# SSD step sizes in the first round of the input projection, with their weights stationary, in a hybrid SSD, Hyena and MoE block

## The chip, the cores and the metric

The kernel runs on one core of a Trainium2 chip. The metric is the device time of one execution in microseconds (us). TensorE multiplies (its weight loads are rows of their own, PEld), VectorE (DVE) and ScalarE (ACT) do elementwise work, GpSimd (POOL) a little of it, SyncE (SP) issues the large DMAs. The engines run their instruction lists in order and meet at semaphores; a list can wait only for its own next instruction.

## The reference, cut to what matters

One layer of a backbone: adaLN-modulated RMSNorm of 256 latent and 256 context tokens of width 2048, one input projection, an SSD (Mamba-2) branch and a Hyena branch, a gated merge, and a mixture of experts. The change touches the SSD step sizes: 64 of the projection's columns (2 directions x 32 heads), a softplus, and the cumulative sums from which all decays come.

```python
def dt_pair(dt_raw, dt_bias):
    bsz, L, _ = dt_raw.shape
    return jax.nn.softplus(dt_raw.astype(F32).reshape(bsz, L, 2, SSD_HEADS) + dt_bias.astype(F32))
...
    dt = dt_pair(p[..., COL_DT:COL_HY], lp['ssd_dt_bias'])
    a = -jnp.exp(lp['ssd_a_log'].astype(F32))
    yf, hf = ssd_chunked(xs, dt[:, :, 0], a[0], bm, cm, h0f)
    yb, hb = ssd_chunked(flip(xs), flip(dt[:, :, 1]), a[1], flip(bm), flip(cm), h0b)
...
    # in ssd_chunked, chunks of 128 tokens
    xd = (xs.astype(F32) * dt[..., None]).reshape(bsz, nc, Q, G, R, P)
    ad = (dt * a).reshape(bsz, nc, Q, G, R).transpose(0, 3, 4, 1, 2)
    acs = jnp.cumsum(ad, axis=-1)
    decay_in = jnp.exp(jnp.where(lower, acs[..., :, None] - acs[..., None, :], -jnp.inf))
    decay_to_end = jnp.exp(acs[..., -1:] - acs)
```

## The kernel before

The program is a row of stages. Each is a block with one instruction list per engine, and between two stages all engines meet at a barrier. No scheduler is at work: the order on each engine is the order in which the code is written. Three stages matter.

**Norm stage (to 127 us).** It leaves the modulated tokens, transposed, as `h_hi` and `h_lo`: fp32 values split into a rounded part and the rest, for 16 tiles of the width (`kt`) and 2 x 256 tokens. A product in full precision is then three matmuls on rounded values, `mm3` (lines 195 to 197): hi with hi, hi with lo, lo with hi.

**xBC projection (127 to 388 us, lines 522 to 680).** Weights come as slabs of 512 KB through 8 slots, `raw`, which SP's `feed` fills as they come free. ScalarE rounds a slab (`split_hi`, L185) into one of 4 places of `w_hi`, which waits for TensorE to have used the slab 4 before (`w_used`). VectorE takes the difference into `w_lo` (`split_lo`, L189), and TensorE waits for that (`lo_ready`). There are 6 rounds of 8 slabs; a round has two parts `p` of 4 slabs, and `project(i, p)` does 24 matmuls of 512 columns for each slab into banks `2p` and `2p + 1`. Then ScalarE copies the two banks out into `p2_pad` (`copy_out`), VectorE convolves (`conv`, L646 and L651), ScalarE applies silu (L601, L603), TensorE transposes (`turn`, L559) into banks 4 to 7 and VectorE copies them to `xb` (`tokens`). The first round is written out (`body(0, first=True)`), rounds 1 to 4 are a hardware loop, and the last round, again written out, has only the 256 latent tokens. In each of these lists the later steps of round i - 1 stand among the splits of round i. VectorE, for one, has slabs 0 to 3, then the steps of the round before, then slabs 4 to 7 and `conv(i, 0)`. SP loads the step weights `wdt` (128 x 16 x 64) at the head of the stage, and does nothing else with them here.

**Scan stage (from 388 us, lines 735 to 1055).** At its head, before any group, stand the step sizes. SP loads the bias, `a_log` and `d` (`bc`). ScalarE rounds `wdt` into place 3 of `w_hi` (L873), VectorE takes the rest (L927). TensorE multiplies with the tokens stationary and the weights moving, 4 tiles of tokens x 16 `kt` x 3 matmuls of 64 columns, so that the steps come out with tokens on the partitions. VectorE and ScalarE take turns for the softplus (L934 to L949, L877 to L881) and leave the steps `dtr` and their product with `a`, `adr` (L951). TensorE multiplies `adr` with triangular tables for the cumulative sums (L783, and L800, L801 for the sums over a whole part), VectorE and ScalarE make exponentials `ex` of them (L957 to L963, L884, L885).

Then a loop over the 4 head groups: copies of the group's part (`bg` L975 and `xsg` L976 on VectorE, `bgt` L889 and `cgt` L890 on ScalarE), small matmuls for states and outputs (L816 to L833), exponentials, mixing (L1024) and 64-column matmuls within a chunk (L854). Between them `ada(part)` reads 32 slabs of `ada_w` in each group (L263, 128x512 with 32 stationary columns): the adaLN rows that later stages need. `feed` refills `raw` for them. ScalarE and GpSimd write these rows out at the end of each group.

Of the kernel before, what the change touches and what calls it, by code (L numbers as in the profile page):

```python
# [199 lines left out]
def build(nc, io, consts):  # L200
    ctx = ExitStack()
    with ctx:
# [102 lines left out]
        with nc.Block() as block:  # L305
# [210 lines left out]
        acc = place("p2_acc", [P, 2, CH_XC], at=after("p2_pad"))  # L516
        s = Box()
        (s.padded, s.conved, s.silud, s.turned, s.tok_copied, s.zeroed,
         s.wdt) = sems(
            "p2", "padded", "conved", "silud", "turned", "tok_copied", "zeroed", "wdt")  # L520

        with nc.Block() as block:

            @block.sync
            def _(sp):
                sp.dma_start(wdt[:], w_in[:, :, COL_DT:COL_HY]).then_inc(s.wdt, 16)
                st.feed(sp, 6, 8, xbc_src, st.lo_ready, lambda j: ada_src(2, j))
                sp.wait_ge(s.wdt, 16)

            @block.gpsimd  # L530
            def _(pool):
                pool.memset(pad[:], 0.0).then_inc(s.zeroed, 1)

            @block.tensor
            def _(pe):
# [3 lines left out]
                def project(i, p, both):  # L539
                    pe.wait_ge(s.padded, i * 4 + 2 * p + 2)  # L540
                    n = 512 if both else L
                    for q in range(4):
# [9 lines left out]
                        mm.then_inc(st.w_used, 1)  # L552

# [17 lines left out]
                body(0, first=True)  # L571
                with pe.Fori(1, 5) as i:
                    body(i)
# [3 lines left out]
            def _(act):  # L577
# [27 lines left out]

                def body(i, first=False, last=False):
# [3 lines left out]
                    for j in (1, 2):  # L610
                        st.split_hi(act, i, 8, j)
                    if not first:
                        copy_out(i - 1, 1, True)
# [4 lines left out]
                    for j in (5, 6):  # L618
                        st.split_hi(act, i, 8, j)
                    copy_out(i, 0, not last)  # L620
                    st.split_hi(act, i, 8, 7)

# [9 lines left out]
            def _(dve):  # L632
# [33 lines left out]

                def body(i, first=False, last=False):
                    for j in range(4):
                        st.split_lo(dve, i, 8, j)
                    if not first:  # L670
                        tokens(i - 1, 0)
                        conv(i - 1, 1, True)
                    for j in range(4, 8):
                        st.split_lo(dve, i, 8, j)
                    if not first:
                        tokens(i - 1, 1)
                    conv(i, 0, not last)

# [35 lines left out]
        wdt_hi, wdt_lo = k.w_hi[:, 3, :], k.w_lo[:, 3, :]  # L714
        xw = place("p3_xw", [P, 6, GC], at=after("wdt"))
        dtr = place("p3_dt", [P, 4, 64], at=after("p3_xw"))
        adr = place("p3_ad", [P, 4, 64], at=after("p3_dt"))
        ex = place("p3_ex", [P, 8, 64], at=hi0 + 3 * 4 * SUB)
# [1710 lines left out]
```

## Time and profile before

| | us |
|---|---|
| median of 3 runs | 2642.38 (2639.52 to 2642.42) |
| the profiled execution | 2643.38 |
| its span, first to last instruction | 2641.6 |
| norm stage ends | about 127 |
| barrier between xBC projection and scan stage | about 388.4 |
| first matmul of the group loop | 453.26 |
| first instruction of the next stage | 652.4 |

Over the whole span TensorE is busy 88% of the time, VectorE 58%, ScalarE 39%, GpSimd 8%, and the mean granted TensorE clock is 0.931 of full speed. These shares are averages over stages with different limits. For this change the timeline of the two stages is to be read, engine by engine, and the windows: for a stretch of the span, how long each engine was busy in it, with how many instructions, the clock that TensorE was granted, the busy share of the 16 DMA engines and what they moved. A granted clock of 1.00 is 2.4 GHz, 0.50 is 1.2 GHz. An fp32 matmul that isn't split into rounded parts stands in the trace as two rows of the same instruction.

### The profile page before, as it was taken

The numbers are of one execution on the slowest core, as the hardware profiler recorded it, in microseconds if no ns is written. First come the engines' busy times: TensorE is split into PE (matmuls) and PEld (weight loads), VectorE is DVE, ScalarE is ACT, GpSimd is POOL, SyncE is SP. The second block draws the span as 40 slices with busy tenths as digits, with TensorE's granted clock in tenths as the row PEclk, the third lists the DMA queues.
The fourth block names the chain that finished last, engine by engine and source line by source line (L and its number), as shares of the span: only waits on it lengthen the run. The fifth ranks groups of instructions, "written<-read, shape, count | busy, mean of one in ns | idle before, by whom it ended". The sixth has DMA issues, their size and how long they took to land. (4 is left out here: it accounts for less than half of the span.)

```text
span 2641.6 us, 34797 instructions
## 1 busy us (share of the span) xinstructions
PE 2334.3 (88%) x12901; PEld 1886.5 (71%) x12901; DVE 1520.1 (58%) x1934; ACT 1032.1 (39%) x1278; POOL 203.6 (8%) x145
## 2 busy tenths in 40 slices
PE   6699988997768798888888999987799999999995
PEld 1288877454658797777777899965588888878773
DVE  1345552565434255767675544453655568989986
ACT  1423321111433242323233333332234446777773
POOL 1000000000000003333333100000000000000000
PEclk9899995998888999999999999998699999999998
DMA  9733320998434553333333456562156668999993
GB/s 370 286 113 93 94 83 22 360 347 308 141 95 155 166 162 100 116 101 116 111 118 105 122 163 183 183 248 59 64 192 191 191 209 320 382 351 365 375 336 129
DMA packets 285401, 503.49 MB, mean 191 GB/s; under 512 B 18757, under 2 KB 158576, under 8 KB 283494
## 3 DMA queue, kind: packets, MB, share of 16 engines
q1 hardware_dynamic: 280310, 481.54, 54.3%
q0 software_dynamic: 4976, 20.43, 2.2%
q8 instruction: 71, 1.16, 0.2%
q14 instruction: 44, 0.36, 0.0%
HBM read 499.78 MB, written 2.13 MB: 190 GB/s over the span
## 5 line engine op out<-in xcount | busy, mean ns | idle before, releaser
L189 DVE TENSOR_TENSOR w_lo<-raw,w_hi 128x1024 fp32r<-128x1024 f32 x720 | 917.8, 1287 | 670.4 <-ACT w_hi L185 643.8
L185 ACT ACTIVATE w_hi<-raw 128x1024 fp32r<-128x1024 f32 x720 | 760.9, 1060 | 842.5 <-PE bank L197 824.4
L195 PE MATMUL bank<-h_hi,w_hi 128*128 128x256 f32 (+1 forms) x1664 | 514.4, 309 | 42.4 <-DVE w_lo L189 29.0
L197 PE MATMUL bank<-h_hi,w_lo 128*128 128x256 f32 (+1 forms) x1664 | 508.1, 305 | 0.0
L196 PE MATMUL bank<-h_lo,w_hi 128*128 128x256 f32 (+1 forms) x1664 | 508.1, 305 | 0.0
L195 PEld LDWEIGHTS bank<-h_hi,w_hi 128*128 128x128 f32 x1664 | 321.0, 193 | 60.0 <-issue 29.5
L196 PEld LDWEIGHTS bank<-h_lo,w_hi 128*128 128x128 f32 x1664 | 320.8, 193 | 14.3 <-issue 1.9
L197 PEld LDWEIGHTS bank<-h_hi,w_lo 128*128 128x128 f32 x1664 | 320.7, 193 | 12.8
L195 PE MATMUL bank<-w_hi,ys_hi 128*128 128x512 f32 x384 | 154.2, 402 | 17.8 <-DVE p_tmp L1855 11.4
L263 PE MATMUL bank<-raw,cpad 128*32 128x512 f32 x768 | 148.9, 671 | 20.5 <-DMA raw<-in_ada_w 20.3
L195 PE MATMUL bank<-ys_hi,w_hi 128*128 128x256 f32 x512 | 148.3, 290 | 17.4 <-ACT merged L1347 10.6
L195 PE MATMUL bank<-w_hi,lt_hi 128*128 128x512 f32 x384 | 154.0, 401 | 2.8 <-DVE w_lo L189 2.8
L196 PE MATMUL bank<-w_lo,ys_hi 128*128 128x512 f32 x384 | 153.5, 400 | 0.0
L197 PE MATMUL bank<-w_hi,ys_lo 128*128 128x512 f32 x384 | 153.4, 399 | 0.0
L197 PE MATMUL bank<-w_hi,lt_lo 128*128 128x512 f32 x384 | 150.0, 391 | 0.0
L196 PE MATMUL bank<-w_lo,lt_hi 128*128 128x512 f32 x384 | 149.7, 390 | 0.0
L196 PE MATMUL bank<-ys_lo,w_hi 128*128 128x256 f32 x512 | 147.4, 288 | 0.0
L197 PE MATMUL bank<-ys_hi,w_lo 128*128 128x256 f32 x512 | 147.4, 288 | 0.0
L195 PE MATMUL bank<-w_hi,hidt_hi 128*128 128x512 f32 x320 | 126.5, 395 | 3.7 <-DVE hidt_lo L2322 2.6
L197 PE MATMUL bank<-w_hi,hidt_lo 128*128 128x512 f32 x320 | 125.3, 392 | 0.0
L196 PE MATMUL bank<-w_lo,hidt_hi 128*128 128x512 f32 x320 | 125.2, 391 | 0.0
L195 PE MATMUL bank<-w_hi,h_hi 128*128 128x512 f32 (+1 forms) x192 | 79.5, 414 | 42.8 <-ACT p_gz L1132 25.1
(358 smaller groups left out, 3103.6 us busy)
## 6 DMA issues: line engine op xcount, KB each, us to landing
raw<-in_w_in SPq DMA_DIRECT2D x240, 512.0 KB, 3.8
raw<-in_ada_w SPq DMA_DIRECT2D x192, 512.0 KB, 7.6
raw<-in_moe_w_gate SPq DMA_DIRECT2D x128, 512.0 KB, 6.0
raw<-in_moe_w_up SPq DMA_DIRECT2D x128, 512.0 KB, 6.0
raw<-in_moe_w_down SPq DMA_DIRECT2D x128, 512.0 KB, 5.9
raw<-in_w_ssd_out SPq DMA_DIRECT2D x32, 512.0 KB, 3.4
raw<-in_w_hy_out SPq DMA_DIRECT2D x32, 512.0 KB, 3.4
raw<-in_w_o SPq DMA_DIRECT2D x32, 512.0 KB, 3.6
```

The source lines that it names most:

```text
L185: act.activation(self.k.w_hi[:, j % HL, :], self.k.raw[:, j % RAW, :], ACT.Copy).then_inc(self.hi_ready, 1)
L189: dve.tensor_tensor(self.k.w_lo[:, j % HL, :], self.k.raw[:, j % RAW, :], self.k.w_hi[:, j % HL, :].bitcast(F32), ALU.subtract).then_inc(s ...
L195: pe.matmul(out, lhs[0], rhs[0], start=start, stop=False)
L196: pe.matmul(out, lhs[0], rhs[1], start=False, stop=False)
L197: return pe.matmul(out, lhs[1], rhs[0], start=False, stop=stop)
L263: mm = pe.matmul(bank[32 * strip:32 * strip + 32, :], k.cpad[:, kt, :], w[:, 0, n * 512:(n + 1) * 512], start=(kt == 0), stop=(kt == KT - 1))
```

## The change

The head of the scan stage moves into the first round of the xBC projection, and the step matmul is turned round.

- SP issues the three loads of `bc` behind that of `wdt`.
- ScalarE rounds `wdt` behind slab 1 into columns 0 to 63 of a new tile `p2_wdt_s` (128 x 16 x 128), VectorE puts the rest into columns 64 to 127.
- TensorE, between slab 0 and slab 1, holds these 128 columns stationary and moves the 512 tokens of `h_hi` and `h_lo` past them: 32 matmuls into bank 5. The outputs stand with steps on the partitions, rounded part and rest apart. VectorE copies the bank out (`dtx`) behind slab 3.
- TensorE, between slab 1 and slab 2, multiplies each 128 tokens of `dtx` with `halves`, two identity matrices one above the other: this adds the two parts and turns them to tokens on the partitions (bank 7). GpSimd makes `halves` from the identity table.
- Softplus behind slab 5 on ScalarE and on VectorE; decay sums between slabs 4 and 5 on TensorE (banks 6 and 7); the rest of the decays at the end of the round on both. TensorE waits for them (`exps`) before round 1.
- The scan stage starts with its group loop; its tiles are placed elsewhere.

```diff
+        wdt_s = place("p2_wdt_s", [P, KT, P], F32R, at=free + 4 * 512)
...
                 sp.dma_start(wdt[:], w_in[:, :, COL_DT:COL_HY]).then_inc(s.wdt, 16)
+                sp.dma_start(bc[:, 0:2, :], io["ssd_dt_bias"].rearrange("a b h -> a (b h)")[0]
...
+                pool.tensor_tensor(halves[:], k.ident[:, 0:64], k.ident[:, 64:P], ALU.add).then_inc(s.zeroed, 1)
...
+                def steps():
+                    pe.wait_ge(s.dt_lo, 1)
+                    for kt in range(KT):
+                        pe.matmul(k.psum[5][:], wdt_s[:, kt, :], k.h_hi[:, :, kt, :], start=(kt == 0), stop=False)
+                        mm = pe.matmul(k.psum[5][:], wdt_s[:, kt, :], k.h_lo[:, :, kt, :], start=False,
+                                       stop=(kt == KT - 1))
+                    mm.then_inc(s.dt_mm, 1)
+
+                def step_tokens():
+                    pe.wait_ge(s.zeroed, 2)
+                    pe.wait_ge(s.dt_sb, 1)
+                    for t in range(4):
+                        mm = pe.matmul(k.psum[7][:, t * 64:(t + 1) * 64], dtx[:, t * P:(t + 1) * P], halves[:],
+                                       start=True, stop=True)
+                    mm.then_inc(s.dt_tok, 1)
+
+                def decay_sums():
+                    pe.wait_ge(s.dts, 1)
+                    out = k.psum[6][:].rearrange("p (n d h) -> p n d h", n=8, d=2)
...
-                    project(i, 0, not last)
+                    project(i, 0, not last, (steps, step_tokens) if first else ())
                     if not first:
                         turn(i - 1, 1)
-                    project(i, 1, not last)
+                    project(i, 1, not last, (decay_sums,) if first else ())
...
                 body(0, first=True)
+                pe.wait_ge(s.exps, 1)
...
+                def step_highs():
+                    act.wait_ge(s.wdt, 16)
+                    act.activation(wdt_s[:, :, 0:64], wdt[:], ACT.Copy).then_inc(s.dt_hi, 1)
...
+                def decay_exps():
+                    act.wait_ge(s.rest, 1)
...
+                def step_lows():
+                    dve.wait_ge(s.dt_hi, 1)
+                    dve.tensor_tensor(wdt_s[:, :, 64:P], wdt[:], wdt_s[:, :, 0:64].bitcast(F32),
+                                      ALU.subtract).then_inc(s.dt_lo, 1)
+
+                def step_copy():
+                    dve.wait_ge(s.dt_mm, 1)
+                    dve.tensor_copy(dtx[:], k.psum[5][:]).then_inc(s.dt_sb, 1)
+
+                def softplus():
+                    dve.wait_ge(s.dt_tok, 1)
+                    dve.wait_ge(s.bc, 48)
...
+                def decay_rest():
+                    dve.wait_ge(s.sums, 1)
...
             def _(pe):
-                pe.wait_ge(s.dt_lo, 1)
-                w = (wdt_hi.rearrange("p (kt n) -> p kt n", n=64), wdt_lo.rearrange("p (kt n) -> p kt n", n=64))
-                for t in range(4):
-                    src, half = t // TT, t % TT
-                    for kt in range(KT):
-                        h = (k.h_hi[:, src, kt, half * P:(half + 1) * P], k.h_lo[:, src, kt, half * P:(half + 1) * P])
-                        mm = mm3(pe, k.psum[0][:, t * 64:(t + 1) * 64], h, (w[0][:, kt, :], w[1][:, kt, :]),
-                                 kt == 0, kt == KT - 1)
-                mm.then_inc(s.dt_mm, 1)
```

Where the order prints names, `p_wdt_s` is the stationary tile, `p_dtx` the copied bank, `p_ad` is `adr`, `p_u` the scratch of the softplus. In the first round on ScalarE, the list before:

```order
L185 ACTIVATE w_hi<-raw 128x1024 [waits w_used,raw_full5]
L185 ACTIVATE w_hi<-raw 128x1024 [waits w_used,raw_full6]
L587 ACTIVATE p_pad<-bank 128x4x64 [waits p2_conved,w_used]
L590 ACTIVATE p_pad<-bank 128x256
L587 ACTIVATE p_pad<-bank 128x4x64
L590 ACTIVATE p_pad<-bank 128x256
L185 ACTIVATE w_hi<-raw 128x1024 [waits w_used,raw_full7]
```

and now, from slab 5 to slab 6 and behind slab 7:

```order
L185 ACTIVATE w_hi<-raw 128x1024 [waits w_used,raw_full5]
L676 ACT_TABLE_LOAD
L676 ACTIVATE p_bc<-p_bc 128x64 [waits p2_bc]
L678 ACTIVATE p_u<-p_dt 128x256 [waits p2_soft]
L680 ACTIVATE p_u<-p_u 128x256 [waits p2_act]
L682 ACT_TABLE_LOAD
L682 ACTIVATE p_u<-p_u 128x256 [waits p2_soft]
L185 ACTIVATE w_hi<-raw 128x1024 [waits w_used,raw_full6]
...
L185 ACTIVATE w_hi<-raw 128x1024 [waits w_used,raw_full7]
L687 ACT_TABLE_LOAD
L687 ACTIVATE p_ex<-bank 128x256 [waits p2_rest]
```

The softplus stands between slabs 5 and 6, and the Exps, which wait for VectorE's `rest`, close the round. On TensorE, what comes into the first round (the plus rows; the matmuls of the projection between them stand as before, and 28 more of the step matmuls are left out):

```order
 L197 MATMUL bank<-h_hi,w_lo 128x512
+L559 MATMUL bank<-h_hi,p_wdt_s 128x512 [waits p2_dt_lo]
+L560 MATMUL bank<-h_lo,p_wdt_s 128x512
...
+L568 MATMUL bank<-p_halves,p_dtx 128x64 [waits p2_dt_sb,p2_zeroed]
+L568 MATMUL bank<-p_halves,p_dtx 128x64 x3
 L195 MATMUL bank<-h_hi,w_hi 128x512 [waits lo_ready]
...
+L579 MATMUL bank<-p_ad,tri 128x32 [waits p2_dts]
+L579 MATMUL bank<-p_ad,tri 128x32 x17
```

Three groups of matmuls now stand between slabs, each behind a wait of its own. On ScalarE at the head of the scan stage and of its group loop, before:

```order
L884 ACT_TABLE_LOAD
L884 ACTIVATE p_ex<-bank 128x256 [waits p3_rest]
L884 ACTIVATE p_ex<-bank 128x128
L885 ACTIVATE p_ex<-p_ex 128x128
L887 UNCONDITIONAL_BRANCH
L887 ISA
L889 ISA [waits p3_ydone]
L889 ACTIVATE p_bgt<-xbc_act 128x256
L890 ISA
L890 ACTIVATE p_cgt<-ct 128x256
```

and now:

```order
L968 UNCONDITIONAL_BRANCH [waits barrier_Pool_Activation_PE_DVE_SP_release]
L971 UNCONDITIONAL_BRANCH
L971 ISA
L973 ISA [waits p3_ydone]
L973 ACT_TABLE_LOAD
L973 ACTIVATE p_bgt<-xbc_act 128x256
L974 ISA
L974 ACTIVATE p_cgt<-ct 128x256
```

The copies follow the barrier directly, and the table load stands inside the loop, behind the group's wait, ahead of its first copy.

## Rows read from the trace of the kernel before

**Rows 1.** Windows: busy us (instructions) of each engine, granted clock, DMA share, GB/s.

```profile
core 0: us, PE busy (x) PEld busy (x) DVE busy (x) ACT busy (x) POOL busy (x), PEclk, DMA share, GB/s
155.00:177.00 22.00, 22.00 (x103) 18.34 (x102) 11.26 (x14) 9.37 (x16) 0.00 (x0) 1.00 0.34 96
...
388.50:432.10 43.60, 41.17 (x192) 41.04 (x192) 1.24 (x2) 2.60 (x3) 1.14 (x2) 0.50 0.01 3
...
440.20:449.80 9.60, 9.55 (x44) 9.46 (x44) 0.00 (x0) 0.00 (x0) 0.00 (x0) 0.50 0.00 0
...
500.00:550.00 50.00, 43.54 (x282) 23.33 (x283) 30.43 (x82) 10.22 (x30) 2.99 (x4) 0.97 0.96 354
```

**Rows 2.** Timeline, head of the scan stage: start, length, engine, work [idle before, releaser].

```profile
388.50 1.06 ACT L873 ACTIVATE w_hi<-wdt 128x1024 fp32r<-128x1024 f32 x1 [0.29 <-PEq L522]
...
432.08 0.42 DVE L934 TENSOR_TENSOR p_dt<-bank,p_bc 128x256 f32<-128x256 f32 x1 [41.27 <-PE bank L197]
...
440.25 7.89 PE L783 MATMUL bank<-p_ad,tri 128*128 128x32 f32 x36 [8.20 <-DVEq L955]
...
451.67 0.41 ACT L890 ACTIVATE p_cgt<-ct 128x256 f32 x1
...
453.26 1.22 PE L816 MATMUL bank<-p_cgt,p_bgt 128*128 128x128 f32 x4 [3.42 <-DVE p_xsg L976]
...
456.60 3.34 SPq L156 DMA_DIRECT2D raw<-in_ada_w  x5
```

**Rows 3.** Timeline of the projection's first round, and the landing time of `wdt`.

```profile
127.02 0.37 SPq L526 DMA_DIRECT2D wdt<-in_w_in  x1
...
DMA to landing us min/median/max: 4.2/4.2/4.2
...
130.51 0.77 PE L195 MATMUL bank<-h_hi,w_hi 128*128 128x512 f32 x1 [24.47 <-DVE w_lo L189]
...
138.21 1.06 ACT L185 ACTIVATE w_hi<-raw 128x1024 fp32r<-128x1024 f32 x1 [6.27 <-PE bank L197]
...
143.65 1.06 ACT L185 ACTIVATE w_hi<-raw 128x1024 fp32r<-128x1024 f32 x1 [4.38 <-PE bank L197]
...
158.73 5.51 DVE L651 SCALAR_TENSOR_TENSOR p_acc<-p_pad,vcol,p_acc 128x528 f32<-128x528 f32 x8
```

**Rows 4.** Timeline: a table load, and the head of the second group.

```profile
433.48 1.28 ACT L881 ACT_TABLE_LOAD   x1
434.77 0.42 ACT L881 ACTIVATE p_u<-p_u 128x256 f32<-128x256 f32 x1
...
500.82 0.40 ACT L890 ACTIVATE p_cgt<-ct 128x256 f32 x1
...
501.33 0.69 DVE L976 COPY p_xsg<-xb 128x1024 f32 x1
...
502.07 0.71 PE L816 MATMUL bank<-p_cgt,p_bgt 128*128 128x128 f32 x4 [2.48 <-DVE p_xsg L976]
```

**Rows 5.** Timeline, TensorE in the first group: two-pass fp32 matmuls of 64 columns.

```profile
481.11 2.00 PE L854 MATMUL bank<-p_xsg,p_mix 128*128 128x64 f32 x16
482.95 0.44 PE L844 MATMUL bank<-tri,p_spans 128*128 128x128 f32 x2
```

**Rows 6.** Timeline, TensorE in the third group; windows of 1 us (columns as rows 1).

```profile
589.49 2.00 PE L854 MATMUL bank<-p_xsg,p_mix 128*128 128x64 f32 x16 [1.35 <-DVE p_mix L1024]
...
592.00:593.00 1.00, 1.00 (x12) 0.27 (x8) 0.14 (x1) 0.00 (x0) 0.00 (x0) 0.50 0.85 336
...
595.00:596.00 1.00, 1.00 (x10) 1.00 (x9) 0.00 (x0) 0.31 (x1) 0.61 (x1) 0.84 0.97 377
...
598.00:599.00 1.00, 0.00 (x0) 0.00 (x0) 0.71 (x2) 1.00 (x4) 0.00 (x0) 0.86 0.69 262
...
605.00:606.00 1.00, 1.00 (x11) 0.12 (x4) 0.29 (x2) 0.00 (x0) 0.00 (x0) 0.72 1.04 422
...
135.00:136.00 1.00, 1.00 (x6) 0.83 (x5) 0.00 (x0) 0.00 (x0) 0.00 (x0) 1.00 1.04 329
```

More of the change, by code:

```diff
@@ new lines, in step_tokens, with total @@
+                def step_tokens():
[8 more added lines that the diff above has]
+                    out = k.psum[6][:].rearrange("p (n d h) -> p n d h", n=8, d=2)
+                    a = adr[:].rearrange("p t (d h) -> p t d h", d=2)
+                    def total(n, d, *terms):
+                        for m, (table, t) in enumerate(terms):
+                            mm = pe.matmul(out[:, n, d, :], table, a[:, t, d, :], start=(m == 0), stop=(m == len(terms) - 1))
+                        return mm
+                    for c in range(TT):
+                        total(c, 0, (k.upper, c))
+                        total(c, 1, (k.lower, c))
+                        total(2 + c, 0, (k.below, c))
+                        total(2 + c, 1, (k.above, c))
+                        for d in range(2):
+                            total(6 + c, d, (k.ones, c))
+                    total(4, 0, (k.upper, 2))
+                    total(4, 1, (k.lower, 2), (k.ones, 3))
+                    total(5, 0, (k.upper, 3), (k.ones, 2))
+                    total(5, 1, (k.lower, 3))
+                    whole = k.psum[7][:, 256:320].rearrange("p (d h) -> p d h", d=2)
+                    for d, (first, second) in enumerate(((3, 2), (2, 3))):
+                        pe.matmul(whole[:, d, :], k.ones, a[:, first, d, :], start=True, stop=False)
+                        mm = pe.matmul(whole[:, d, :], k.ones, a[:, second, d, :], start=False, stop=True)
+                    mm.then_inc(s.sums, 1)
@@ L540, in project @@
+                def project(i, p, both, between=()):
                     pe.wait_ge(s.padded, i * 4 + 2 * p + 2)
@@ L611, in body @@
                         st.split_hi(act, i, 8, j)
+                        if first and j == 1:
+                            step_highs()
                     if not first:
@@ L669, in body @@
                         st.split_lo(dve, i, 8, j)
+                        if first and j == 1:
+                            step_lows()
                     if not first:
@@ L672, in body @@
                         conv(i - 1, 1, True)
+                    else:
+                        step_copy()
                     for j in range(4, 8):
                         st.split_lo(dve, i, 8, j)
+                        if first and j == 5:
+                            softplus()
                     if not first:
@@ L677, in body @@
                     conv(i, 0, not last)
+                    if first:
+                        decay_rest()
                 body(0, first=True)
```

167 lines of the change are left out of this document (71 added, 96 removed).

## The prediction, made before the changed kernel was run

> **What bounds the kernel now.** I read the timeline by engine first, at the place that the change empties: the start of the scan stage (the SSD block, from 388.5 us). ScalarE rounds the step weights at 388.50, VectorE can add the bias to the steps only at 432.08, behind 192 matmuls of 64 columns, the decay sums run from 440.25, and the first matmul of the group loop comes at 453.26 [rows 1, 2]. In all that time nothing else is due on any engine: it is one chain, handed from engine to engine. The windows say what else is idle: over 388.5 to 432.1 the DMA share is 0.01, inside the group loop it is 0.96 at 354 GB/s [rows 1]. The loop streams 128 slabs of `ada_w`; its first refill leaves at 456.60 [rows 2], because all 8 slots of `raw` are full and the loop is what first reads them. So the loop's end is set by a stream that begins when the loop begins: whatever brings the loop forward brings its end forward by as much.
>
> The stage that receives the work, the xBC projection (127 to 388 us), is bound by TensorE: 22.00 of 22.00 us busy from 155 to 177 at full clock, with VectorE at 11.3 and ScalarE at 9.4 us [rows 1]. ScalarE's rounding waits for a released slot every 5.44 us (138.21 to 143.65), that is for 24 matmuls of 512 columns at 0.2267 us [rows 3]. Work put on TensorE here costs its full time; work on the other two costs nothing while they stay ahead.
>
> **The change, part by part. (1) The head of the scan stage goes.** After the barrier each engine walks straight into the group loop. One thing is new, seen in the instruction order: the table load for Exp, which stood ahead of the loop, now stands at the head of each group, before ScalarE's first copy. A table load took 1.28 us, and the next ScalarE instruction began 1.29 us after its start [rows 4]. The two copies end 0.72 us after the first begins (0.31 us before the row at 451.67, 0.41 from there on). ScalarE: 388.50 + 1.29 + 0.72 = 390.5, so TensorE starts at about 390.6; VectorE's copies alone, 0.34 + 0.69 us, would have allowed 389.6. Gain 453.26 - 390.6 = **62.7 us**.
>
> In groups 2 to 4 the load costs again. Today TensorE's row at 502.07 waits for VectorE's copy at 501.33 (0.69 us), while ScalarE's at 500.82 ends at 501.2 [rows 4]; with 1.29 more ScalarE ends at 502.5, so TensorE starts 0.5 us later, at a place where slabs are in flight. Between 0 (they cover it) and 3 x 0.5 = 1.5; I take 0.5.
>
> The Trainium skill (ScalarE: Activation LUTs, section What ACT_TABLE_LOAD costs) puts a switch of tables at about 2.66 us, a load of 1.28 and a drain of 1.38. By that each of the four heads would lose 1.4 us more, and the sum would be up to 5.6 us worse. The row at 434.77 begins 1.29 us after the load's start, without a drain, so the measurement decides here.
>
> **(2) Step matmuls.** 4 x 16 x 3 = 192 matmuls, whose time was that of loading weights, become 32 with 512 columns, between slab 0 and slab 1 of the first round. They have the form of the projection's: 32 x 0.2267 = **7.3 us**, all on the path. Their weights: `wdt` lands 4.2 us after 127.02 [rows 3], at 131.2; ScalarE's rounding (1.06, as at 388.50) ends by 132.4 and VectorE's rest by 133.7, while TensorE ends slab 0 at 138.1: 4.4 us to spare. Slabs 2 and 3, which these two push back by some 3 us, are wanted only from 151 on. SP issues three small loads behind `wdt`, each about as long as that one's 0.37, and is through by 128.7; its feed can't act before slab 0 is split, which also lets TensorE begin at 130.51. Nothing moves.
>
> **(3) Turning the steps to tokens.** Four fp32 matmuls of 64 columns, two passes each. Such passes ran 16 in 1.84 us, 481.11 to 482.95 [rows 5], 0.115 each: 8 x 0.115 = **0.9 us**. VectorE's copy of the bank ahead of them has slab 1's 5.4 us to be done in.
>
> **(4) Decay sums.** 22 fp32 matmuls of 32 columns, 44 passes. The trace has them only at half clock, 44 in 9.55 us [rows 1]. At full clock the nearest row is that of the 64-column passes [rows 5], set by the same weight load: 44 x 0.115 = **5.1 us**. Their input: VectorE's chain took 8.2 us from its row at 432.08 to the sums' start at 440.25 [rows 2]. It can begin once slab 5 is split, which hangs on TensorE's release of slab 1 at 150.8: ScalarE to 152.0, VectorE to 153.3, so the input is ready at 161.5. TensorE comes to the sums at about 168 (five slabs, 7.3 and 0.9): nothing waits, with 6.5 us to spare.
>
> **(5) The clock.** In the group loop full clock is lost without a long idle stretch: 1.35 us of waiting and 1.9 us of 64-column passes (589.49), then 0.50 in 592 to 593 and back within 595 to 596. After the next gap it falls within 598 to 599 and comes back within 605 to 606 [rows 6]. The decay sums are 5.1 us of passes with half as many columns, so I expect such a fall there though TensorE never stops. The two stretches at the low level lasted about 3.3 and 6.7 us, and every us of projection at half clock does half its work. The cost is 0 if the clock does not fall, and up to 4.4 (all 44 passes in 9.5) + 3.3 = 7.7 if it falls at once. I take the long stretch at half loss: **3.3 us**.
>
> **(6) What is queued behind the new waits.** VectorE runs the softplus before slabs 6 and 7 and the first convolution; ScalarE waits for `rest` before slab 8 and the first silu. In order: VectorE splits slab 6 by 162.7; slab 7, released at 162.6 and rounded after four short copies (some 1.3 us, by 0.4 us copies such as at 500.82), by 166.0; the convolution takes 1.0 + 5.5 us (158.73) [rows 3], to 172.6; `decay_rest` follows the sums (173 to 178), ScalarE's Exps end by 179, slab 8 by 181.4, table load and four silus by 184. TensorE needs slab 8 and these silus after slab 7, at 189.5 or later. Cost **0**, with 5 us to spare; with that cover gone, every us of lateness would be a us.
>
> **Sum.** -62.7 + 7.3 + 0.9 + 5.1 + 3.3 + 0.5 = -45.6 us. The profiled execution took 2643.4 (its span and 1.8 around it), 1.0 above the median of the three runs. 2643.4 - 45.6 = 2597.8, in terms of the median **2597** (-1.7%).
>
> **Rivals.**
> A. The clock does not fall at the sums. For it: in the projection the transposes, 0.8 us of small matmuls, leave it at 1.00 [rows 1]. Against: rows 6. Time 2597 - 3 = **2594**.
> B. The clock falls early and the seam of part 6 turns late: the sums take 9.5 instead of 5.1 us, and `rest` moves to the end of its range; the first transposes then wait some 2 us, and the group heads lose all of their 1.5. 2597 + 4.4 + 2 + 1 = **2604**.
> C. The stream is not what ends the loop, and an earlier start only moves a wait. If half of the head's 62.7 us came back in it: 2597 + 31 = **2628**. Against: with a DMA share of 0.01 the head leaves the loop nothing but 8 full slots, and these are as full without it.
> D. The change doesn't do what it says: an engine's first step in the loop still waits for the chain. It would give back up to the whole gain, **2642**. Against: TensorE enters its second round only behind `exps`, so no part of the chain is left by the barrier.
> E. Slower: the clock, once down at the sums, stays down. In the head it held 0.50 while TensorE was busy 41.17 of 43.6 us [rows 1], on 64-column matmuls. Were 512 columns no better, some 35 full slabs at 5.44 us more each and 8 half ones at half that would add about 210 us: **2800**. It decides from 9 slabs (49 us) at the low level on. Against: the stage starts at the low level too, and 135 to 136 shows 1.00 [rows 6], before slab 0 ends.
>
> **Chances.** Forecast 0.60, A 0.17, B 0.15, C 0.03 (all faster), D 0.02 (same), E 0.03 (slower). A measurement of this kernel tells about 0.2%, 5 us, from no change. Faster 0.95, same 0.02, slower 0.03. The range goes down to A with 4 us for a cheaper part 2 and a loop that starts earlier, 2590, and up to B with 2 us more, 2606; C, D and E and the tails lie outside.
>
> **What would show it.** After the change the group loop's first matmul stands some 2.4 us after the barrier, and the barrier about 16.6 us later than before; 32 step matmuls stand at 0.227 us, the sums turn from 0.115 to about 0.215 a pass with the granted clock at 0.5 for some us behind them; TensorE has no gap between 130.5 and the end of the stage; the four groups are as long as before at the same DMA share. Wrong would be: TensorE waiting for `dt_lo`, `dts` or `silud` in the first round, groups longer by over a us each, or a clock that stays low past the first round.

## The result, and the profile after

| | us |
|---|---|
| before, 4 runs beside it | 2642.4 (2639.52 to 2647.30) |
| changed kernel, 4 runs | 2602.1 (2599.65 to 2604.97) |
| ratio, 95% interval | 0.9846 (0.9827 to 0.9865) |
| the profiled execution, and its span | 2600.52, 2598.6 |

All times here are of executions at the usual granted clock, from 0.93 to 0.945 over the span; one of 2765.4 us, among the six of the kernel with both mends below, ran at 0.812 and is left out.

The time, 1.5% shorter, lies inside the range of 2590 to 2606, 5 us above the forecast of 2597. The profiled execution is 42.9 us shorter than that of before, where the sum had 45.6.

First the page's head for the changed kernel: the busy time, its share and the instructions of each engine.

```profile
## 1 busy us (share of the span) xinstructions
PE 2297.8 (88%) x12749; PEld 1846.2 (71%) x12749; DVE 1521.2 (59%) x1935; ACT 1037.3 (40%) x1282; POOL 204.1 (8%) x146
```

TensorE has 36.5 us less work than before (2334.3 us then): the 41 us of small matmuls have become 8, with the turn. The shares have hardly moved, so they say nothing about where the time went. The timeline does. It follows for the first round of the projection; it answers to [rows 2] and [rows 3]. Columns are as there: start, length, engine, line, work, and in brackets the idle time before and who ended it.

```profile
131.37 0.77 PE L195 MATMUL bank<-h_hi,w_hi 128*128 128x512 f32 x1 [24.48 <-DVE w_lo L189]
...
132.14 1.06 ACT L672 ACTIVATE p_wdt_s<-wdt 128x1024 fp32r<-128x1024 f32 x1 [1.22 <-DMA wdt<-in_w_in]
133.23 1.22 DVE L759 TENSOR_TENSOR p_wdt_s<-wdt,p_wdt_s 128x1024 fp32r<-128x1024 f32 x1 [0.86 <-ACT p_wdt_s L672]
...
139.01 0.39 PE L559 MATMUL bank<-h_hi,p_wdt_s 128*128 128x512 f32 x1
...
146.26 0.39 PE L195 MATMUL bank<-h_hi,w_hi 128*128 128x512 f32 x1
...
151.70 1.00 PE L568 MATMUL bank<-p_halves,p_dtx 128*128 128x64 f32 x8
152.51 0.48 PE L195 MATMUL bank<-h_hi,w_hi 128*128 128x512 f32 x1
...
161.83 0.42 DVE L788 SCALAR_TENSOR_TENSOR p_ad<-p_dt,p_bc 128x256 f32<-128x256 f32 x1
...
168.96 4.10 PE L579 MATMUL bank<-p_ad,tri 128*128 128x32 f32 x36
...
174.15 0.77 PE L195 MATMUL bank<-h_hi,w_hi 128*128 128x512 f32 x1
...
191.82 1.03 PE L622 MATMUL bank<-tri,xbc_act 128*128 128x128 f32 x8
```

The differences of starts give the price of each insertion: steps 146.26 - 139.01 = 7.25 us, turn 152.51 - 151.70 = 0.81, sums 174.15 - 168.96 = 5.19. Behind the first, none of TensorE's rows has a bracket: it never waits. Their inputs are early, `wdt_s` by 4.6 us (134.45 against 139.01), `adr` by 6.7 (162.25 against 168.96). What TensorE waits for between 127 and 410 us, as the list of waits has it (total, times, longest):

```profile
PE bank L195 <- DVE w_lo L189: 24.5, 1, 24.5
PE bank L913 <- ACT p_cgt L974: 8.5, 1, 8.5
```

These are the stage's start and the loop's start, and nothing between. The silus that the first transposes (191.82) need ended at 181.0, 11 us ahead. The granted clock behind the sums, in windows of 1 us (columns as rows 1):

```profile
173.00:174.00 1.00, 1.00 (x9) 1.00 (x8) 0.49 (x1) 0.00 (x0) 0.00 (x0) 0.70 0.00 0
174.00:175.00 1.00, 1.00 (x4) 0.90 (x4) 0.56 (x3) 0.00 (x0) 0.00 (x0) 0.50 0.00 0
...
176.00:177.00 1.00, 1.00 (x4) 0.81 (x3) 0.43 (x1) 1.00 (x1) 0.00 (x0) 0.59 0.00 0
```

By the shares of 173 to 174 and 176 to 177 it fell to 1.2 GHz at 173.4, 4.4 us after the sums began, with TensorE busy all the time, and was back at 176.8 (the next window shows 1.00).

At the head of the loop, ScalarE and TensorE, for [rows 2] and [rows 4]:

```profile
404.86 1.28 ACT L973 ACT_TABLE_LOAD   x1 [0.86 <-DVEq L1009]
406.16 0.42 ACT L973 ACTIVATE p_bgt<-xbc_act 128x256 f32 x1
406.48 0.40 ACT L974 ACTIVATE p_cgt<-ct 128x256 f32 x1
406.93 1.23 PE L913 MATMUL bank<-p_cgt,p_bgt 128*128 128x128 f32 x4 [8.49 <-ACT p_cgt L974]
...
452.93 0.60 ACT L1004 ACTIVATE p_arow<-bank 128x512 f32<-128x512 f32 x1 [6.54 <-PE bank L263]
455.66 1.28 ACT L973 ACT_TABLE_LOAD   x1 [2.13 <-DVEq L1097]
456.96 0.42 ACT L973 ACTIVATE p_bgt<-xbc_act 128x256 f32 x1
...
457.73 1.22 PE L913 MATMUL bank<-p_cgt,p_bgt 128*128 128x128 f32 x4 [2.96 <-ACT p_cgt L974]
```

The loop begins 46.3 us earlier than before. In the second group TensorE now waits for ScalarE, 2.96 us where it was 2.48 [rows 4], since the table load stands ahead of the copies: 4.80 us from the start of the `arow` copy that ends a group to the next group's first matmul, where it was 4.32. And the loop as a whole, from its first matmul to its fourth `arow` copy, takes 196.1 us where it took 190.3. The windows of its groups 2 to 4, before and then after, show where (the first group took 44.5 and takes 46.0):

```profile
497.80:545.40 47.60, 43.21 (x281) 22.99 (x281) 28.76 (x78) 8.32 (x23) 2.41 (x3) 0.96 0.96 351
545.40:594.70 49.30, 44.75 (x281) 23.08 (x281) 28.76 (x78) 8.37 (x23) 2.41 (x3) 0.94 0.97 356
594.70:643.60 48.90, 44.62 (x282) 23.79 (x282) 28.77 (x78) 8.40 (x24) 2.41 (x3) 0.92 0.93 337
```

```profile
452.90:502.40 49.50, 44.49 (x281) 23.37 (x282) 28.77 (x78) 9.66 (x24) 2.42 (x3) 0.93 0.93 344
502.40:552.60 50.20, 45.11 (x281) 23.12 (x282) 28.76 (x78) 9.65 (x24) 2.40 (x3) 0.93 0.94 347
552.60:603.00 50.40, 45.42 (x281) 23.39 (x281) 28.77 (x78) 9.66 (x24) 2.52 (x3) 0.90 0.91 335
```

Each group is 0.9 to 1.9 us longer, at a lower DMA share (0.91 to 0.94 where groups 2 to 4 had 0.93 to 0.97), with TensorE busy longer for the same instructions, at a lower mean clock but for group 3's 0.94 and 0.93, which hardly differ. Of the 5.8 us, 1.5 lie in the first group, which holds no later head. This is the part that the prediction had at 0.5 us, and the experiments begin with it.

### The profile page after: what moved, and what is told of

It reads as the page before. It is cut to its first block and busy times, and to the rows that moved or that the text cites. A ratio compares the mean times of both kernels' runs of the same rounds, so it can differ in the third digit from the quotient of the medians.

```text
span 2598.6 us, 34493 instructions
## 1 busy us (share of the span) xinstructions
PE 2297.8 (88%) x12749; PEld 1846.2 (71%) x12749; DVE 1521.2 (59%) x1935; ACT 1037.3 (40%) x1282; POOL 204.1 (8%) x146
## 5 line engine op out<-in xcount | busy, mean ns | idle before, releaser
L195 PE MATMUL bank<-w_hi,ys_hi 128*128 128x512 f32 x384 | 154.1, 401 | 17.8 <-DVE p_tmp L1900 11.4
L196 PE MATMUL bank<-w_lo,lt_hi 128*128 128x512 f32 x384 | 149.6, 389 | 0.0
L195 PEld LDWEIGHTS bank<-ys_hi,w_hi 128*128 128x128 f32 x512 | 99.7, 195 | 19.0 <-issue 11.8
```

What stands on the lines that cost most here:

```text
L195: pe.matmul(out, lhs[0], rhs[0], start=start, stop=False)
L196: pe.matmul(out, lhs[0], rhs[1], start=False, stop=False)
```

## The experiments

Two theories stood at the start. **The loaded head**: the table load in the loop delays TensorE by some 0.5 us at each group, and in a loop that lives on its stream this costs several times its own length. The rival, **the other phase**: the loop only begins at another moment relative to the clock, the barrier and the filled slots, and is longer or shorter for that, table load or not. Beside them, two questions: what the fall of the clock costs, and which half of the change, turning or moving, brings the gain. All ratios are against the kernel before on the same chip.

**The loop without the load.** One Exp on a single column ahead of the loop makes the compiler put the load there.

```diff
             def _(act):
+                act.activation(k.small[:, 60:61], k.ident[:, 0:1], ACT.Exp)
                 act.sem_inc(s.ada_row, 1)
```

> The changed kernel with one Exp on a single column ahead of the group loop, so that the table load stands outside the loop again. The group loop of the changed kernel takes 196.1 us from its first matmul to its fourth row of adaLN copies, that of the kernel before 190.3. Theory 1 (the load at each group's head delays TensorE by 0.5 us, lengthens its gap and so lets slabs pile up and the clock fall more often): the heads go back from 4.8 to 4.3 us between the adaLN copy and the next group's first matmul, the loop to 190 to 192, the total 4 to 5 us below the changed kernel. Rival 2 (the stream of slabs ran slower in that execution, for reasons outside the program): heads shorter by 0.5 us, 1.5 in all, the loop still at 194 or more, total within 2 us of the changed kernel.

Measured: 2596.5 us (2595.3 to 2602.9, 5 runs), ratio 0.9813 (0.9800 to 0.9825). The profiled execution is the longest of the five. ScalarE at the loop's start:

```profile
405.42 1.28 ACT L970 ACT_TABLE_LOAD   x1 [0.56 <-PEq L533]
406.71 0.20 ACT L970 ACTIVATE small<-tri 128x1 f32<-128x1 f32 x1
406.82 0.40 ACT L974 ACTIVATE p_bgt<-xbc_act 128x256 f32 x1
```

The load is there once, and at the end of the first group ScalarE goes from `arow` (453.66) to `p_bgt` (456.40) without one. The heads are 4.3 to 4.5 us again and the loop takes 192.2.

**The load brought into the loop of before.** The same the other way: a Silu on one column between the head and the loop of the kernel before.

```diff
                 act.activation(ex[:, 4:6, :], ex[:, 4:6, :], ACT.Exp).then_inc(s.exps, 1)
+                act.activation(k.small[:, 60:61], k.ident[:, 0:1], ACT.Silu)
                 act.sem_inc(s.ada_row, 1)
```

> The kernel before with one Silu on a single column between the head of the scan stage and its group loop, which puts the Exp table load at the head of each group. The head gets longer by 2.8 us (two loads and the Silu). Theory 1: the loop gets longer by 4 to 6 us too, the total is 7 to 9 us above the kernel before. Rival 2: the loop gets longer by 1.5 us at most, total 3 to 4 us above.

Measured: 2650.0 us (2644.7 to 2655.9, 12 runs), ratio 1.0019 (1.0011 to 1.0028), 4.7 us over the 2645.3 of before there. The profiled execution has the loop at 195.1 us (4.8 more), the heads at 4.8, and its first matmul 3.05 us later, behind two loads:

```profile
452.74 1.28 ACT L886 ACT_TABLE_LOAD   x1
...
454.24 1.28 ACT L890 ACT_TABLE_LOAD   x1
...
456.31 1.22 PE L816 MATMUL bank<-p_cgt,p_bgt 128*128 128x128 f32 x4 [5.22 <-ACT p_cgt L891]
```

The loop does what the first theory says. The median rose by less than the 7 to 9 us expected and by more than the rival's 3 to 4. The two profiled executions do differ by the parts: 2652.04 - 2643.38 = 8.7 us, which are 3.05 (0.7 of it a later start of the projection), 4.8 and 0.8 behind the loop. The difference from 4.7 is where the two lie in their own runs: that of before 1.9 us under the median on this chip, this one 2.1 over its own.

**The changed kernel once more**, beside those two, for what repeats.

> The changed kernel once more, on the chip of the others. If its loop takes 196 us again, within 1 us, its length belongs to the program; if it comes out at 190 to 193, the stream's rate varies between executions and the 5.8 us are in part such a variation.

Measured: 2603.7 us (2602.1 to 2607.9, 5 runs), ratio 0.9843 (0.9830 to 0.9856); loop 195.9 us, heads 4.8. So the Exp ahead brings 7.2 us in the medians on this chip, and the intervals of the two ratios do not overlap. The two traces show only part of it: the loop is 3.6 us shorter, but the profiled execution with the Exp took 2602.9 us, 6.4 above its median, with 3.7 us more behind the loop. From the first step matmul to the first transposes it takes 54.4 us here (138.88 to 193.30), where the first trace has 52.8 (139.01 to 191.82): the clock stayed low behind the sums for 6.8 us, from 173.15 to 179.97, and not for 3.4.

**A delay without a load.** Is it the load, or any lateness of ScalarE? The Exp stays ahead of the loop, and at each head ScalarE makes four useless copies of 256 columns between its two.

```diff
+                act.activation(k.small[:, 60:61], k.ident[:, 0:1], ACT.Exp)
...
+                    for n in range(4):
+                        act.activation(dec[:, n // 2, 2 * (n % 2):2 * (n % 2) + 2, :].rearrange("p h n -> p (h n)"),
+                                       k.xbc_act[:, ds(g, 1), 0:L].rearrange("p a n -> p (a n)"), ACT.Copy)
```

> The changed kernel with Exp ahead of the loop (no table load in it), and in place of the load four more copies of 256 columns on ScalarE at the head of each group, 4 x 0.31 = 1.24 us, results unused. Theory 1 (any 0.5 us more of gap at a head costs that much): heads at 4.8 us again, loop 195 to 197, total as the changed kernel's. If the table load costs something besides its time, the loop stays at 192 to 193 with heads of 4.8.

Measured: 2603.8 us (2599.6 to 2606.5, 4 runs), ratio 0.9838 (0.9824 to 0.9853).

```profile
452.40 0.60 ACT L1008 ACTIVATE p_arow<-bank 128x512 f32<-128x512 f32 x1 [6.54 <-PE bank L263]
455.14 0.42 ACT L974 ACTIVATE p_bgt<-xbc_act 128x256 f32 x1 [2.15 <-DVEq L1101]
455.47 1.32 ACT L976 ACTIVATE p_dec<-xbc_act 128x256 f32 x4
```

Heads of 4.74 us, loop of 196.1: the same as with the load. It is the lateness, not the table. Against the Exp ahead alone the total is higher too, by ratio 0.9838 to 0.9813, though their intervals just touch.

**The sums in two halves.** 20 passes behind slab 4, 24 behind slab 5 (10 and 12 matmuls; the expectation has them the other way round), everything else as in the changed kernel.

```diff
-                    project(i, 1, not last, (decay_sums,) if first else ())
+                    project(i, 1, not last, (lambda: decay_sums(0), lambda: decay_sums(1)) if first else ())
```

> The changed kernel with the decay sums in two parts, 24 passes behind slab 4 and 20 behind slab 5. In the changed kernel the clock fell after 4.6 us of these passes and came back 3.2 us later, at a price of 1.6 us. If small matmuls alone bring it down, by their running on for that long, it stays at full level here: 44 passes take 4.9 to 5.1 us and nothing behind them is slow, total 1.6 us lower. If the fall has another cause (a wait, the moment in the stage), it falls again. The seam: the sums end 5.4 us later, the silus before the first transposes at 186, TensorE needs them at 191; no wait.

Measured: 2600.9 us (2595.3 to 2601.6, 4 runs), ratio 0.9824 (0.9809 to 0.9838), against 0.9843 for the changed kernel on that chip; these two intervals overlap, so the total alone doesn't settle a gain. The two halves in the timeline, and a window between them, which shows full clock, as do all from 167 to 184:

```profile
169.50 2.31 PE L580 MATMUL bank<-p_ad,tri 128*128 128x32 f32 x20
...
177.22 1.86 PE L580 MATMUL bank<-p_ad,tri 128*128 128x32 f32 x16
```

```profile
174.00:175.00 1.00, 1.00 (x6) 0.80 (x6) 0.03 (x1) 0.00 (x0) 0.00 (x0) 1.00 0.00 0
```

The second row leaves out the last 8 passes, of other lines: the halves take 2.15 us (to 171.65) and 2.59 (to 179.81), 4.7 together. From the first step matmul to the first transposes it is now 51.3 us (139.54 to 190.83): the fall cost 52.8 - 51.3 = 1.5 us in the first trace and 3.1 in the second, of which 0.45 within the sums themselves. The other traces fall in line: 52.8 with the copies in the loop, 54.4 with the Exp ahead, and 51.3 twice more in the two kernels below that have the sums in two. The loop, whose heads still have the load, takes 196.1.

**Turning alone.** The kernel before, with the step matmul turned round at its old place at the head of the scan stage (stationary tile, copy, `halves`; softplus, sums and all else stay there).

```diff
-                for t in range(4):
-                    ...
-                        mm = mm3(pe, k.psum[0][:, t * 64:(t + 1) * 64], h, (w[0][:, kt, :], w[1][:, kt, :]),
-                                 kt == 0, kt == KT - 1)
+                for kt in range(KT):
+                    pe.matmul(k.psum[5][:], wdt_s[:, kt, :], k.h_hi[:, :, kt, :], start=(kt == 0), stop=False)
+                    mm = pe.matmul(k.psum[5][:], wdt_s[:, kt, :], k.h_lo[:, :, kt, :], start=False,
+                                   stop=(kt == KT - 1))
```

> The kernel before with the step matmul turned round (weights stationary, 32 matmuls of 512 columns, a copy, 4 fp32 matmuls with the two identities), but still at the head of the scan stage. There 192 matmuls took 41.2 us at the low clock. 32 take 13.7 us if the clock stays low, 9 to 11 if it rises on the way; copy 0.7, turn 0.9 to 1.7. So 25 to 30 us below the kernel before, and the move alone is worth the other 13 to 17 of the 41.

Measured: 2616.9 us (2612.3 to 2619.9, 4 runs), ratio 0.9897 (0.9883 to 0.9911), 28.1 us below before.

```profile
390.69 0.79 PE L774 MATMUL bank<-h_hi,p_wdt_s 128*128 128x512 f32 x1 [8.22 <-DVE p_wdt_s L934]
...
396.83 0.41 PE L774 MATMUL bank<-h_hi,p_wdt_s 128*128 128x512 f32 x1
...
424.30 1.22 PE L823 MATMUL bank<-p_cgt,p_bgt 128*128 128x128 f32 x4 [3.42 <-DVE p_xsg L985]
```

The 41 us of 64-column matmuls have become 10.3 (390.69 to 401.0). They started at the low clock, and their length fell from 0.63 to 0.40 at 396.8: with 512 columns TensorE gets its clock back, which the 64-column form at the same place did not. The loop starts 29.0 us earlier.

**Moving alone.** The changed kernel, with the old 192 matmuls of 64 columns in the place of the 32, in the first round.

```diff
-                        pe.matmul(k.psum[5][:], wdt_s[:, kt, :], k.h_hi[:, :, kt, :], start=(kt == 0), stop=False)
-                        ...
+                            mm = mm3(pe, k.psum[7][:, t * 64:(t + 1) * 64], h, (wdt_s[:, kt, 0:64], wdt_s[:, kt, 64:P]),
+                                     kt == 0, kt == KT - 1)
```

> The changed kernel with the step matmul in its old form (tokens stationary, 192 matmuls of 64 columns) between slab 0 and slab 1, no turn behind it. At full clock the weight load sets 0.115 to 0.12 us each, 22 to 23 us in place of 8.1: 15 above the changed kernel. But the decay sums lost the clock after 4.6 us of such matmuls; if 64 columns do the same, most of the 192 run at 0.2146, up to 41 us, and slab 1 begins at the low level: 30 to 36 above the changed kernel, and then to move them would have been worth little over the kernel before.

Measured: 2635.1 us (2630.2 to 2640.3, 6 runs), ratio 0.9964 (0.9952 to 0.9977), 9.9 us below before. Windows, and the first matmul of slab 1 behind the block:

```profile
142.00:143.00 1.00, 1.00 (x10) 1.00 (x9) 0.00 (x0) 0.00 (x0) 0.00 (x0) 0.86 0.46 45
145.00:150.00 5.00, 5.00 (x25) 5.00 (x25) 0.00 (x0) 0.00 (x0) 0.00 (x0) 0.50 0.00 0
...
180.00:181.00 1.00, 1.00 (x5) 0.83 (x4) 0.00 (x0) 0.00 (x0) 0.00 (x0) 0.86 0.00 0
```

```profile
175.95 0.77 PE L195 MATMUL bank<-h_hi,w_hi 128*128 128x512 f32 x1
```

The block began at 138.76 at full clock, lost it at 142.7 (the length of its matmuls goes from 0.28 to 0.40 there) and kept 0.50 to its end at 175.95, 37.2 us in all; the clock came back at 180.3, 4.3 us into the 512-column matmuls. So moving alone is worth 10 us, turning alone 28, and the two together 40 to 42 (the changed kernel and its repeat).

**Sums back at the scan stage.** Steps and softplus stay in the first round; sums, `rest` and Exps go back to the head of the scan stage, and with them the table load leaves the loop.

```diff
-                    project(i, 1, not last, (decay_sums,) if first else ())
+                    project(i, 1, not last, ())
...
             def _(pe):
+                decay_sums()
                 with pe.Fori(0, GROUPS) as g:
```

> The changed kernel with only steps and softplus in the first round; decay sums and what follows stand at the head of the scan stage as before (Exp ahead of the loop with them, so no table load in the loop). Moved back: 44 passes at the low level, 9.5 us, the rest 0.9, the Exps 1.4 with their load hidden, against 5.2 plus 1.1 to 2.5 of clock in the first round: the loop's first matmul comes 5 to 6 us later than in the changed kernel (first matmul of the projection to first of the loop: 281 us instead of 275.6). The loop is 4 to 6 us shorter, without the load. Total within 2 us of the changed kernel. If the loop stays at 196, theory 1 is wrong about the table load.

Measured: 2599.8 us (2597.9 to 2604.3, 4 runs), ratio 0.9839 (0.9824 to 0.9854).

```profile
396.43 7.86 PE L859 MATMUL bank<-p_ad,tri 128*128 128x32 f32 x36 [5.87 <-PEq L533]
...
409.42 1.22 PE L893 MATMUL bank<-p_cgt,p_bgt 128*128 128x128 f32 x4 [3.42 <-DVE p_xsg L1020]
```

The loop's first matmul stands 279.2 us behind the projection's first, where the changed kernel has 275.6: moving the sums gained 3.6 us (2.1 against the repeat, where the clock stayed low longer). But with the Exps ahead of it the loop takes 190.0, some 6 us less. As the changed kernel does it, its last step costs about as much as it gains: 0.9839 against its 0.9843 and 0.9846.

**Both mends together**: the Exp ahead of the loop, and the sums in two halves.

> The changed kernel with both edits: one Exp ahead of the group loop and the decay sums in two parts. If the two effects are apart from each other (7 us for the loop, 1 to 2.5 us for the clock behind the sums), about 8 to 9 us below the changed kernel on the same chip, 2594 to 2596. If they overlap, no better than the first alone (2596 to 2597 on the chip of before, where the changed kernel took 2603.7).

Measured: 2594.6 us (2591.4 to 2596.2, 5 runs), ratio 0.9808 (0.9795 to 0.9820). Loop 189.4 us, heads 4.3. By the ratios that is some 9 us below the changed kernel, but only about 1 us below the Exp alone (0.9813), well within the intervals: a gain from the sums in two on top of the Exp is seen in the trace behind them, not in the total.

**Heads shorter still.** Of that kernel, the first matmul of a group waits only for ScalarE's copies, not for VectorE's copy of `xsg`, which it doesn't read.

```diff
-                    dve.tensor_copy(xsg[:], k.xb[:, 0:TT, ds(g * GC, GC)]).then_inc(s.staged, 1)
+                    dve.tensor_copy(xsg[:], k.xb[:, 0:TT, ds(g * GC, GC)])
...
-                    pe.wait_ge(s.staged, g * 2 + 2)
+                    pe.wait_ge(s.staged, g + 1)
```

> The version with Exp ahead of the loop and the sums in two parts, and at each group's head TensorE waits only for ScalarE's two copies, which its first matmuls read, not for VectorE's copies. Heads 4.3 us become 3.5 to 3.6. Theory 1 (each half us of gap at a head costs 1 to 2 us of loop, by the clock and by slabs standing full) gives a loop of 185 to 188 where it was 189.4, total 2 to 4 us below that version (2590 to 2593). If the loop is by then set by the stream alone, it stays at 188 to 190 and the total within 1 us of it.

Measured: 2594.6 us (2592.2 to 2594.9, 5 runs), ratio 0.9812 (0.9799 to 0.9826).

```profile
454.26 1.22 PE L919 MATMUL bank<-p_cgt,p_bgt 128*128 128x128 f32 x4 [1.68 <-ACT p_cgt L981]
```

TensorE waits 0.8 us less at each head (1.68 where it was 2.50), heads of 3.51 us, and the loop takes 189.2: nothing is gained, and the first theory's 185 to 188 did not come. Its weight loads wait for slabs 20.1 us in all, in 22 places, where the kernel above has 17.2 in 18.

**The loops side by side**, of each profiled execution. "Low clock" is summed from windows of 1 us, two times what each lacks to 1.00; "DMA lack" sums what the DMA share lacks to 1.00 behind the first 7 us.

| kernel | heads | loop | low clock | DMA lack |
|---|---|---|---|---|
| changed | 4.8 | 196.1 | 29.8 | 18.6 |
| changed, once more | 4.8 | 195.9 | 27.6 | 18.8 |
| sums in two | 4.8 to 4.9 | 196.1 | 31.3 | 20.4 |
| copies in the loop | 4.74 | 196.1 | 28.3 | 19.0 |
| before, load in the loop | 4.8 | 195.1 | 28.7 | 15.9 |
| moving alone | 4.8 | 192.2 | 20.7 | 16.1 |
| Exp ahead | 4.3 to 4.5 | 192.2 | 24.2 | 16.7 |
| before | 4.3 to 4.7 | 190.3 | 22.6 | 13.1 |
| sums at the scan stage | 4.3 | 190.0 | 18.4 | 13.8 |
| both mends | 4.3 | 189.4 | 17.9 | 12.5 |
| shorter heads | 3.5 | 189.2 | 17.8 | 14.2 |
| turning alone | 4.3 | 187.5 | 10.1 | 12.1 |

Late heads: 195.3 us on average; the others 189.8. The two sets touch at 192.2, and within each the loops differ by 4 to 5 us, so the phase has a say too; but the average difference of 5.5 us follows the heads, in kernels whose loops start at moments from 405 to 456 us. It lies where the heads are: the first groups average 45.7 and 45.4 us, groups 2 to 4 together 149.6 and 144.4. And it is mostly stream time missed: the loop less its DMA lack is 175 to 179 us in all twelve, and the lack averages 18.1 with late heads, 13.7 with the others. How 0.5 us becomes 1.7 for each group is seen some 6 to 8 us behind the `arow` copy. Windows there, behind the second and the last head of before, and then behind the second and third heads of the changed kernel:

```profile
552.00:553.00 1.00, 1.00 (x8) 0.22 (x4) 1.00 (x3) 0.00 (x0) 0.00 (x0) 0.50 0.64 256
...
601.00:602.00 1.00, 1.00 (x8) 0.20 (x4) 1.00 (x3) 0.00 (x0) 0.00 (x0) 0.50 0.14 53
```

```profile
510.00:511.00 1.00, 1.00 (x8) 0.21 (x4) 1.00 (x6) 0.00 (x0) 0.00 (x0) 0.50 0.19 59
...
559.00:560.00 1.00, 1.00 (x8) 0.20 (x4) 1.00 (x3) 0.70 (x3) 0.00 (x0) 0.50 0.02 8
```

SP's first loads behind the pause, at the second head of before and at the third of the changed kernel:

```profile
552.02 0.99 SPq L156 DMA_DIRECT2D raw<-in_ada_w  x2
```

```profile
560.59 0.82 SPq L156 DMA_DIRECT2D raw<-in_ada_w  x2
```

While TensorE is away at a head, and then slow at the low clock, few slabs come free, all 8 slots fill, and the queues run dry. SP's longest pause between two loads was 5.5, 5.4 and 7.0 us at the three heads of before (the second from 546.66 to 552.02), 6.9, 6.3 and 7.2 in the changed kernel (the third from 553.43 to 560.59). Before has a dry spot behind a head, a window with a DMA share under 0.2, only at its last, which is also its latest (4.66 us); the changed kernel has one at all three. It isn't a strict rule: moving alone has heads of 4.8 us, a dry spot behind only one of them, and a loop of 192.2. Both kernels also have a dry window some 30 us into a group (528 and 576 before, 485 and 584 after), and the changed kernel one at 434 to 436 in its first group, where no head is late; the heads are not the only place. Whether the longer gap lowers the clock for longer and that dries the stream, or the dry stream makes the gaps that hold the clock down, no run here separates.

## Why the prediction was right, and where its sum was off

**The mechanism held.** The head was one chain, the loop's stream starts when the loop starts, and the gain is the shift of that start: predicted 46.1 us (without the 0.5 for the heads), measured 46.3. That these agree to 0.2 us is in part luck: the norm stage ended 0.9 us later in this execution (131.37 against 130.51), the head gave 0.6 less, and the clock cost 1.8 less than its term. In the repeat, where the clock cost 3.1, the shift is 44.9. The barrier came 15.9 us later, where 16.6 were forecast.

**Part 1, the head:** 62.7 predicted. Before, 64.8 us lay between the barrier (388.4) and the loop's first matmul; after, 2.65. That is 62.1. TensorE waits for ScalarE behind the table load there, as the trace after shows. The next ScalarE instruction begins 1.30 us after the load's start (404.86 to 406.16), so the drain that the prediction weighed and left out doesn't show.

**Part 1, the group heads:** this is the step that failed. One of the prediction's own signs of being wrong came true here: three of the four groups are longer by over a us. The prediction had the mechanism (ScalarE's load now ends last, TensorE starts 0.5 us later; measured 0.48) and "a place where slabs are in flight", and took from that that they would cover it, 0.5 us with 1.5 as the end. The measured term is 5.8 us in the trace (1.5 of it in the first group), 5.5 on average over the loops, and 7.2 in the medians of the same kernel with and without it. I had argued that the loop's end is set by its stream, and then counted lateness of TensorE as hidden by the stream or at most worth itself. A stream through 8 slots is fed only by TensorE's releases, so lateness at a head stops the stream as soon as all slots are full. The range of the term had to reach to what a dry stretch costs, 2 us for each group; the dry spot at 601 to 603 us of before was there to be read.

**Parts 2 to 4:** steps 7.3 against 7.25, turn 0.9 against 0.81, sums 5.1 against 5.19. Durations of the same form in the same state of the clock carry over to 0.1 us. For the sums the agreement is luck: at full clock throughout, in two halves, the 44 passes took 4.7 us (0.108 each, not the 0.115 of the 64-column row), and the fall within them added 0.45.

**Part 5, the clock:** 3.3 predicted, 1.5 measured in this execution and 3.1 in the repeat (the sums in two halves are the control). It fell as rows 6 suggested, but only when the sums were nearly over, and was back after 3.4 us here and after 6.8 in the repeat: both stretches of rows 6 occur, and the forecast's choice of the long one fits the repeat. Rival A, no fall, was wrong.

**Part 6, the seam:** 0, and with 11 us to spare where I had 5, because softplus and Exps kept well ahead. One detail was wrong without effect: the issue of the first `bc` load took SP 1.40 us, not 0.37, and SP was through with the three at 130.64 and not at 128.7. Its feed has to wait for the split of slab 0 in any case, and began at 131.49, 0.12 us behind TensorE's first matmul, as it did before (130.62 and 130.51).

**The sum again:** start +0.9, parts 2 to 4 +13.2, clock (beyond the 0.45 within the sums) and the rest of the stage +1.7, head -62.1, loop +5.8, and -2.4 from the loop's end on: -42.9. The last term is luck of this execution: the repeat has 1997.5 us behind the loop, this one 1995.6, before 1998.1. The forecast had -45.6. The other 2.6 us of the 5 by which the median missed are where the two profiled executions lie in their own runs (1.0 above the median before, 1.6 below it after). Rival B came closest in its number, 2604, but by other parts: neither its early fall of the clock nor its late seam took place. C was wrong in its mechanism, though it asked the right question; what came back in the loop was 6 us of 62. D and E had no part. The time lies inside the range although the heads' term, with 1.5 as its end, did not reach what they cost; smaller clock cost and the shorter rest made room for it.

Against rival E the clearest answer is that of the old form moved: after 33 us at the low level, 512-column matmuls had full clock back in 4.3 us, where 64-column ones had kept 0.50 for all that time.

## What to carry to other kernels

Work that stands alone in front of a stream-bound loop is worth its full time if it can be done in an earlier stage that is bound by one engine, at that engine's price; here that price was 37.2 us with 64 columns for each weight load, and 8.1 with 512 and the turn. In this loop the moments at which the consumer is away were not covered by the stream but multiplied, up to a point: look for windows whose DMA share goes to zero, and count new lateness at these places several times, but don't expect a gain from less lateness where no window is dry. When a function of another table set is moved away from ahead of a loop, see in the instruction order where the table load went: one dummy instruction ahead of the loop took it out again, for 7 us in the medians.

## What the runs showed of the hardware

- TensorE lost full clock while it was busy without a gap: 4.4 us after the start of the 32-column sums, 4.0 us after that of the old 64-column form in the first round, where it stayed at 1.2 GHz for the remaining 33 us. The sums split into 2.15 and 2.59 us, with a slab of 512-column matmuls between, left the clock at 1.00. The Trainium skill (TensorE: Matmul & The Clock Gate, section Why this matters for your kernels) names idle gaps between bursts of matmuls as what makes throughput drop in mid-kernel; by that neither stretch would have lost the clock, and the runs differ.
- 512-column matmuls brought full clock back each time: 4.3 us after the old form's block, and 6.1 us into the turned step matmuls at the head of the scan stage, where 192 matmuls of 64 columns had stayed at 0.50 for 41 us.
- A table load cost 1.30 us from its start to the next instruction's (404.86 to 406.16, 455.66 to 456.96): the first behind silus, the second in a loop whose only ScalarE functions are Exp and Copy. It stands ahead of a Copy in each turn of that loop, though no other table was asked for since the turn before.
- A lateness of 0.45 us at three heads of a stream-bound loop went with 5.5 us; 0.8 us less lateness than before brought nothing. Heads of 4.7 us and more went with loops of 192.2 to 196.1 us, heads of 4.3 to 4.7 with 187.5 to 192.2; from 4.3 us down to 3.5 the loop stayed at 189. The loop less its DMA lack hardly moved, 175 to 179 us.
